# A hybrid decoder layer on one core: the attention's work one step apart, and the meta tile's weighted sums as split products

## The reference, cut to what matters

```python
def dsa_block(qpos, q_lat, q_idx, w_idx, c_kv, k_idx, topk):
    ...
    _, sel = lax.top_k(score, topk)                      # the 128 best keys of each query
    ...
    s = jnp.einsum('bqhc,bqkc->bqhk', q_lat, kv_sel).astype(jnp.float32) * (ATT_HEAD_DIM ** -0.5)
    ...
    p = jax.nn.softmax(s, axis=-1).astype(c_kv.dtype)
    return jnp.einsum('bqhk,bqkc->bqhc', p, kv_sel)      # weighted sums of the latents
...
y_att = jnp.einsum('bthc,hcd->bthd', o_lat, w_uv).reshape(bsz, t_len, ATT_WIDTH)
```

## Time and profile before

| | us |
|---|---|
| median of three runs | 1017.67 |
| the profiled execution's own time | 1017.49 |
| its span, first to last instruction | 1015.8 |
| PE busy (matmuls) | 996.9 (98%) |
| PEld busy | 907.9 (89%) |
| DVE busy | 714.0 (70%) |
| ACT busy | 493.8 (49%) |
| POOL busy | 118.1 (12%) |
| attention's steps on PE, 527 to 600.6 | 73.6 |

### The profile page before, as it was taken

The page is one execution under the profiler, slowest core; times in us unless marked ns, Lnnn a source line. Parts: engine busy times, 40 slices in busy tenths (PEclk is TensorE's granted clock), DMA queues, the critical chain, the costliest instruction groups (busy, mean ns, idle before and its releaser), DMA issues.

```text
span 1015.8 us, 18999 instructions
## 1 busy us (share of the span) xinstructions
PE 996.9 (98%) x7028; PEld 907.9 (89%) x7028; DVE 714.0 (70%) x1317; ACT 493.8 (49%) x868; POOL 118.1 (12%) x92
## 2 busy tenths in 40 slices
PE   9999999999999999999999999999999999999996
PEld 8999999999999988699765668889999999988886
DVE  6988888887322264699997523699989889942236
ACT  6656665566121264546346522576656665812121
POOL 0000000001121262045302205320000000000000
PEclk9999999999999999999999999999999999999999
DMA  7233332323223313132110102113323232333212
GB/s 252 84 100 107 102 105 90 116 80 105 86 86 111 113 44 116 36 123 82 44 42 1 43 1 83 43 42 126 124 83 124 85 121 96 125 103 101 98 57 84
DMA packets 30849, 90.48 MB, mean 89 GB/s; under 512 B 4689, under 2 KB 5329, under 8 KB 30801
## 3 DMA queue, kind: packets, MB, share of 16 engines
q1 hardware_dynamic: 30800, 89.83, 26.7%
HBM read 87.72 MB, written 2.10 MB: 88 GB/s over the span
## 4 chain that ended last, share of the span: by engine, by line
PE 81%; DVE 15%; ACT 2%; issue 1%; DMA 0%; SPq 0%; DVEq 0%; ACTq 0%
PE ps L1229 38%; PE ps L1287 22%; PE ps L1152 9%; DVE sc L2201 3%; DVE top L2200 3%; PE ps L1714 2%; PE ps L1424 1%; PE ps L1692 1%; DVE qk L2240 1%; PE ps L1705 1%; DVE wlo L1877 1%; PE ps L1489 1%; PE ps L1722 1%; PE ps L1337 1%; PE ps L1335 1%
## 5 line engine op out<-in xcount | busy, mean ns | idle before, releaser
L1229 PE MATMUL ps<-tsum,whi 128*128 128x264 f32 (+1 forms) x1280 | 243.1, 282 | 0.5 <-ACT ht L790 0.5
L1229 PEld LDWEIGHTS ps<-tsum,whi 128*128 128x128 f32 x1280 | 202.3, 188 | 0.7 <-issue 0.7
L1229 PE MATMUL ps<-tsum,wlo 128*128 128x264 f32 (+1 forms) x640 | 180.3, 282 | 0.0
L1229 PE MATMUL ps<-xh,whi 128*128 128x264 f32 (+1 forms) x480 | 135.4, 282 | 0.3 <-ACT sil L790 0.3
L1229 PE MATMUL ps<-xl,whi 128*128 128x264 f32 (+1 forms) x480 | 135.5, 282 | 0.0
L1229 PE MATMUL ps<-xh,wlo 128*128 128x264 f32 (+1 forms) x480 | 135.3, 282 | 0.0
L729 ACT ACTIVATE whi<-wraw 128x1408 fp32r<-128x1408 f32 (+1 forms) x48 | 74.6, 1555 | 123.0 <-PE ps L1287 123.0
L1787 DVE TENSOR_TENSOR wlo<-wraw,whi 128x1408 fp32r<-128x1408 f32 (+1 forms) x38 | 70.0, 1843 | 85.3 <-ACT whi L729 85.3
L1287 PE MATMUL ps<-hh,whi 128*128 128x264 f32 (+1 forms) x462 | 124.2, 323 | 0.0
L1287 PE MATMUL ps<-hh,wlo 128*128 128x264 f32 (+1 forms) x462 | 123.5, 322 | 0.0
L1287 PE MATMUL ps<-hl,whi 128*128 128x264 f32 (+1 forms) x462 | 123.4, 321 | 0.0
(11 more groups left out here) (287 smaller groups left out, 1828.0 us busy)
## 6 DMA issues: line engine op xcount, KB each, us to landing
wraw<-in_ffn_w_gate SPq DMA_DIRECT2D x43, 512.0 KB, 4.2
wraw<-in_ffn_w_up SPq DMA_DIRECT2D x42, 512.0 KB, 4.3
wraw<-in_ffn_w_down SPq DMA_DIRECT2D x32, 384.0 KB, 3.2
wraw<-in_ffn_w_down SPq DMA_DIRECT2D x32, 320.0 KB, 3.5
wraw<-in_w_in SPq DMA_DIRECT2D x19, 512.0 KB, 4.5
wraw<-in_w_out SPq DMA_DIRECT2D x8, 512.0 KB, 4.4
out<-zrow SPq DMA_DIRECT2D x8, 256.0 KB, 2.0
x<-in_x SPq DMA_DIRECT2D x3, 528.0 KB, 7.5
```

What stands on the lines that cost most here:

```text
L1229: mm = pe.matmul(ps[:, bank, 0:(HT, HALF_SEQ)[p // 2]], w[:, k * P:(k + 1) * P], v[:, k, :], start=(first and k == 0 and n == 0), stop=(k ...
```

## The change

Two things are changed, both in the attention and its preparation.

The meta tile's sum W0 becomes a split product. ACT copies T0's weights (now 32 rows are turned, of which the last 16 belong to tile 1) into an fp32r buffer; DVE subtracts that from the PSUM value and puts the low part 32 partitions below. PE then runs two fp32r products in place of one fp32 product: the latents' low part by the high weights, and a 64-row tile, which holds the latents' high part twice, by the stacked high and low weights. ACT makes the latents' high part ahead of the attention, before the `hi` of weight unit 4; POOL makes their low part and the 64-row tile after its low part of weight unit 9.

The order of the steps is moved. Score 4G+2 and 4G+3 stand between the turns and sums of group G-1; of the tail of a query tile, `project` and `normalise` stay in the steps 3, 5 and 7, and `turn_y`, `att_hi` and `att_lo` go to the steps 4, 6 and 8. `normalise`, `att_lo`, the mLSTM heads' steps and the late rounds stand behind mask 4G+3 on DVE; on ACT the copies of T0 and T1 stand before the exps, one by one, and `att_hi` behind the last.

The diff, cut:

```diff
-HEAD_GATED = ((1, 0), (1, 1), (2, 1), (3, 1))
+HEAD_GATED = (1, 1, 2, 3)
-LATE_AT = ((4, 0), (4, 1), (5, 0))
+LATE_AT = (4, 4, 5)
...
+META_ROWS = 32
...
+                def split_latents():
+
+                    pool.wait_ge(c_hi, 1)
+                    pool.wait_ge(ct_turned, 1)
+                    m = N_META
+                    pool.tensor_tensor(clo[0:m, 0, :], cmat[0:m, 0, :], chi[0:m, 0, :].bitcast(F32), ALU.subtract).then_inc(c_lo, 1)
+                    link(pool.memset(meta_c[:, :].bitcast(F32), 0.0))
+                    for e, r in enumerate((0, 32)):
+                        pool.wait_ge(c_lo, e + 1)
+                        pool.tensor_copy(meta_c[r:r + m, :], chi[0:m, 0, :].bitcast(F32)).then_inc(c_lo, 1)
+                    pool.wait_ge(c_lo, 3)
...
                 act.activation(ct[:, END[3]:T], ps[:, 5, 0:P], ACT.Copy).then_inc(ct_ready, 1)
+                act.activation(chi[0:N_META, 0, :], cmat[0:N_META, 0, :], ACT.Copy).then_inc(c_hi, 1)
                 hi(MIX0 + 4, 0, UW, False)
...
                 for G in range(GROUPS + 1):
-                    for half in range(2):
+                    last_tile = 1 + (G - 1) // 2
+                    if G >= 1:
+                        copy_odd(G - 1, (0, 1))
+                    for q in range(4):
                         if G < GROUPS:
-                            exps(G, (2 * half, 2 * half + 1))
...
+                            exps(G, (q,))
+                        if G >= 1 and 2 + q <= last_tile:
+                            copy_odd(G - 1, (2 + q,))
+                    if turned_late is not None:
+                        att_hi(turned_late)
...
                 def weigh(G, i):
                     t = TP0[G] + i
-                    pe.wait_ge(pt_even if t % 2 == 0 else pt_odd, t // 2 + 1)
-                    if i == 0 and G >= 1:
-                        pe.wait_ge(ol_ready, G)
-                    pe.matmul(ps[:, 3, :], cmat[0:ROWS[i], i, :], pt_flat[0:ROWS[i], (t % 2) * 512:(t % 2 + 1) * 512],
-                              start=(i == 0), stop=(i == 1 + G // 2)).then_inc(pv_step, 1)
+                    if i == 0:
+                        pe.wait_ge(pt_hi, copies_by_act(t))
+                        if G >= 1:
+                            pe.wait_ge(ol_ready, G)
+                        pe.wait_ge(c_lo, 3)
+                        m = N_META
+                        pe.matmul(ps[:, 3, :], clo[0:m, 0, :], pt_h[t % 2][0:m, :], start=True, stop=False)
+                        copied_weights(t)
+                        pe.matmul(ps[:, 3, :], meta_c[:, :], pt_h[t % 2][0:64, :], start=False, stop=False).then_inc(pv_step, 1)
+                        return
+                    copied_weights(t)
+                    pe.matmul(ps[:, 3, :], cmat[:, i, :], pt[t % 2], start=False, stop=(i == 1 + G // 2)).then_inc(pv_step, 1)
...
+                    if G < GROUPS:
+                        scores(4 * G)
+                        scores(4 * G + 1)
+                    if G == 0:
+                        turn_mlstm((0, 1))
                     if G >= 1:
+                        turn(G - 1, 0)
+                        turn(G - 1, 1)
+                    if late is not None:
+                        project(late)
+                    if turned_late is not None:
+                        turn_y(turned_late)
+                    if G < GROUPS:
+                        scores(4 * G + 2)
+                    if G >= 1:
+                        weigh(G - 1, 0)
+                        if last_tile >= 2:
+                            turn(G - 1, 2)
+                            weigh(G - 1, 1)
...
-                            dve.tensor_copy(pt_flat[0:ROWS[i], 0:512], ps[0:ROWS[i], 0, :]).then_inc(pt_even, 1)
+                        if i == 0:
+                            dve.wait_ge(pt_hi, copies_by_act(t))
+                            ins = dve.tensor_tensor(pt_h[t % 2][32:32 + META_ROWS, :], ps[0:META_ROWS, t % 2, :],
+                                                    pt_h[t % 2][0:META_ROWS, :].bitcast(F32), ALU.subtract)
...
+                    if late is not None:
+                        normalise(late)
+                    if turned_late is not None:
+                        att_lo(turned_late)
+                    if G in (0, 2):
+                        normed_mlstm((2 + G // 2,))
+                    for h in range(ML_H):
+                        if HEAD_GATED[h] == G:
+                            gated_mlstm((h,))
+                    late_rounds(G)
```

More of the change, by code:

```diff
@@ L1730, in turn_y @@
                     mm.then_inc(yt_turned, 1)
-                late = None
+                late, turned_late = None, None
                 for G in range(GROUPS + 1):
                     last_tile = 1 + (G - 1) // 2
[L1735 to L1746, removed]
-                    if G >= 1:
-                        for i in range(last_tile + 1):
-                            if 2 <= i + 1 <= last_tile:
-                                turn(G - 1, i + 1)
+                    if G < GROUPS:
[3 more added lines that the diff above has]
+                        turn_mlstm((0, 1))
+                    if G >= 1:
+                        turn(G - 1, 0)
[11 more added lines that the diff above has]
+                            weigh(G - 1, 1)
+                        if last_tile >= 3:
+                            turn(G - 1, 3)
+                    if G < GROUPS:
+                        scores(4 * G + 3)
+                    if G >= 1:
+                        for i in range(1 if last_tile < 2 else 2, last_tile + 1):
@@ L1751, in attention @@
                             weigh(G - 1, i)
+                            if 4 <= i + 2 <= last_tile:
+                                turn(G - 1, i + 2)
                         if G in (1, 2):
                             turn_mlstm((G + 1,))
-                        if late is not None:
-                            turn_y(late)
-                        late = last_tile if (G - 1) % 2 else None
+                        turned_late, late = late, last_tile if (G - 1) % 2 else None
                 pe.wait_ge(yml_lo, ML_H)
@@ L2369, in copy_even @@
                                 dve.wait_ge(pv_step, t - 1)
[L2370 to L2375 removed]
+                            ins = dve.tensor_copy(pt[t % 2], ps[:, t % 2, :])
+                        else:
+                            continue
@@ L2377, in attention, with late_rounds @@
+                        ins.then_inc(pt_lo, 1)
+                def late_rounds(G):
+                    for n, at in enumerate(LATE_AT):
+                        if at == G:
+                            select(4, LATE_ROUND + n, LATE_ROUND + n + 1)
+                turned_late = None
                 for G in range(GROUPS + 1):
                     last_tile = 1 + (G - 1) // 2
[L2379 to L2392, removed]
@@ L2393, in attention @@
-                    if G >= 1:
[L2394 to L2398, removed]
+                    if G < GROUPS:
+                        masked(4 * G)
+                        masked(4 * G + 1)
+                    if G >= 1:
+                        copy_even(G - 1, range(min(last_tile, 2) + 1))
```

80 lines of the change are left out of this document (52 added, 28 removed).

## The result

The changed kernel takes 1020.31 us (median of 11 runs, 1019.40 to 1021.25) where the kernel before took 1017.90 beside it (11 runs, 1017.17 to 1018.41): a ratio of 1.0022 [1.0013, 1.0031]. A second comparison on another chip gave 1.0025 [1.0016, 1.0034]. It is slower by 2.4 us where 2.55 less was forecast, and lies above the range. The profiled execution took 1019.83, with a span of 1018.1.

The account below looks back on a forecast made before the run. The attention was taken as bound by PE's own list. 4.2 (split) + 2.9 (old waits) - 4.35 (new waits) - 0.2 (mixer) = 2.55 us less, giving 1015.1; forecast's own range 1013.6 to 1016.6, whole range 1012.0 to 1018.8.

Parts of the forecast that it names:

- split pair: W0's two fp32r products on PE: 0.54 us in place of 1.06, 4.2 less over eight; bounds 0.5 to 4.8.
- wait C: Step 5 on PE: score 22 waits for mask 20, behind att_lo and two rounds on DVE; 1.6 us, bounds 0 and 4.
- wait A: W0's second product on PE waits for ACT's copy, then DVE's subtraction; 1.6 us over all steps, bounds 0 and 5.5.
- wait B: Ends of steps 1 and 2: turn_mlstm on PE waits for DVE's mLSTM pieces; 0.4 and 0.75, together 1.15 us.
- the prediction's own sign, a pair of 0.8 or more: Stated sign of being wrong: W0's two products on PE cost 0.8 us or more.
- The old waits on ACT's copies: PE's waits in the attention before, claimed removed: 1.8 us in step 4, 2.9 in all with three others.
- The mixer's 0.2: In the mixer, ACT's 16x128 copy stands ahead of the `hi` DVE waits for; costs 0.2 us, at most 0.27.
- Waits in its place: Rival: new PE waits of 6.45 us replace the fp32 work, leaving 0.45 less, 1017.2 us; chance 0.20.
- DVE's block: Rival: DVE's work at the steps' ends becomes the bound; new waits 10.75, 3.85 slower, 1021.5 us; chance 0.09.
- The pair at its upper bound: Rival: W0's two products cost 1.0 us, saving 0.5 in place of 4.2; 1.15 slower, 1018.8 us; chance 0.05.
- The contention that the prediction weighed and left out: DVE's threshold at 495.11 could wait for a small POOL instruction on shared ports; some 0.3 us, sum 2.25 not 2.55.

Follow-up runs that it names:

- the last experiment: W0 made one fp32r product of 128 rows, against the changed kernel with late rounds and two mLSTM pieces moved on DVE: 1010.77 us, 0.9933 of the kernel before.

## Why the prediction was wrong

The sum of the forecast for the attention was 4.2 + 2.9 - 4.35 = 2.75 less; the trace has 1.95 more. Term by term:

| term | forecast | trace | worse by |
|---|---|---|---|
| split pair, 8 times | 1.06 to 0.54 | 1.06 to 0.85 | 2.5 |
| the clock's fall behind wait C | not seen | 1.5 (2.3 in the median) | 1.5 |
| wait A | 1.6 | 1.22 | -0.4 |
| wait B | 1.15 | 0.66 + 1.06 = 1.72 | 0.6 |
| wait C | 1.6 | 1.77 | 0.15 |
| score 26 in step 6 | 0 | 0.28 | 0.3 |
| sum | | | 4.65 of 4.7 |

**The first step that failed** is "I take 0.54, as PE has only one fp32 to fp32r step per pair". The mechanism at its upper end, each product with its weight load uncovered, was the right one, at 0.85 and not 1.0; the prediction's own sign, a pair of 0.8 or more, is met. Rows 6 all have 128 rows. W0 against W1 in fp32 was read by durations, 1.12 and 1.02, and these run past the next start. From start to start W0 costs 1.06, and W1, in step 5 of the kernel before, 0.86:

```profile
567.31 1.02 PE L1714 MATMUL ps<-v,cs 128*128 128x512 f32 x2
568.17 0.60 PE L1705 MATMUL ps<-ident,qi 128*128 128x128 f32 x4
```

That is 0.20 more for W0, about one load, so the number of rows did matter. A nearer row was in the trace of before and I did not look it up: an fp32r product of 36 rows among others of 128.

```profile
456.44 0.50 PE L1590 MATMUL ps<-parted,picks 36*128 36x512 f32 x1
456.87 0.39 PE L1424 MATMUL ps<-whi,xh 128*128 128x256 f32 x1
```

It costs 0.43 where one of 128 rows costs 0.23 to 0.31, the 0.42 to 0.43 of each of the pair. With it the forecast would have been 1017.6, no change. The Trainium skill (TensorE: Matmul & The Clock Gate, section "Step-by-step: what each phase is for") has weight loads pulled ahead of running products where the row groups don't conflict or the load goes to a background buffer; the loads of the last experiment agree (0.13 apart). Those of 16 and 64 rows weren't pulled ahead (0.24 of waiting), and no run here shows which of the two conditions was missing. It also says that the row count doesn't matter to the length of a load, and there the rows agree: 0.18 for 16 and for 64, 0.19 for 128.

**The second** is "So PE stands for 1.6": the length was right (1.77), but a stand of PE was priced as time and nothing more. That the granted clock was 1.00 in the attention before was taken over for the attention after; it was read where PE's longest bracket was 1.01. In the changed kernel a bracket of 0.90 in step 2 was followed by no fall, the 1.53 in step 5 by one in each of its profiles. The two experiments with work in the wait show that the fall hangs on it, and the one with six products shows 2.3 us as its price.

**What held.** The old waits on ACT's copies went (no bracket names them), every wait that was forecast is where it was put, released by what was named, and all but B within 0.4; B was short by 0.3 in each of its steps, since the mask begins 0.2 after W1 (542.78 and 542.58), where I let both begin together, and W1 is 0.86 and not 0.96. The experiments that moved DVE's pieces confirm B and C as PE's own time; A was only read from the trace. The mixer's 0.2 came to 0.37 at the first score, but 0.26 of it was there before ACT's copy; the part that is the change's is about 0.1.

**The rivals.** "Waits in its place" asked for 6.45 us of new waits, and there are 5.0. "DVE's block" came nearest in time, with 1021.5, but by chance: it asked for 10.75 us of new waits. "The pair at its upper bound", 1018.8 with 0.05 of the chance, came nearest in mechanism. The fall of the clock, which made the kernel slower than before, stood in none of them.

## What to carry to other kernels

Price a product by a row with its own number of rows and the neighbours' rows. Here an fp32r product of 16, 36 or 64 rows between products of other numbers of rows cost 0.42 to 0.43, as its weight load stood open; and one product padded to 128 rows, with more terms in the empty rows, cost 0.31 where the pair cost 0.85. Count a new wait on PE twice, as time (1.77 here) and as a chance that the clock falls behind it (2.3); short work in the wait tells the two apart. When an order is moved by a step, look at what then stands ahead of the first mask on DVE: here moving three rounds and two small pieces turned a loss of 2.4 us into a gain of 3.6.

## What the runs showed of the hardware that was not expected

The fall of the clock is not the same in each execution: behind the same wait it lay at 0.70 and 0.96 in one profile and at 0.51 and 0.81 in another of the same kernel, 1.5 and 2.9 us (from score 22 to W2, 565.51 to 571.56 and 564.66 to 572.03, against the 4.52 of the same work at 1.00 in the kernel with six products). What makes it longer stays open. So does what it takes beside a stand: behind the brackets of 1.01 and 0.90 the clock stayed at 1.00. The Trainium skill (the same page, section "HAM oscillation — how this bites in real kernels") has a kernel that runs at the lower clock again after each wait for data; here the lower clock came once, behind a wait for DVE, in a stretch otherwise full.

The contention that the prediction weighed and left out is there, and small: in the changed kernel the threshold at 495.38 began 0.07 behind the second of POOL's two copies of 16 rows (495.31) and took 0.45, where it took 0.37 at 495.11 before. That is 0.08 more, against 0.3 as the estimate by that rule. The other runs bear it out: the threshold takes 0.45 to 0.47 in all seven profiles in which it begins just behind that copy, and 0.37 in the three without the copies. In the kernel with one product of 128 rows it begins first (495.04) and takes 0.37, and the copy behind it, at 495.11, takes 0.46 in place of 0.28. So whichever began second was held up; whether it stood for the whole of the other's time, no run here tries by itself.
